# Five groups of split-number tiles begin 64 bytes further on in the on-chip memory

## The reference

```python
for layer in range(DEPTH):                    # 2
    if layer % 2 == 0:
        x = x + mixer_ab(x, ...)              # gated recurrence and pooling, then @ w_out (1536 rows)
    else:
        x = x + conformer_conv(x, ...)        # @ w1, depthwise conv, layer norm, silu, then @ w2
    x = x + cross_attn(x, mem, ...)           # 4 heads over 256 memory rows, then @ wo
    x = x + conv_ffn(x, ...)                  # (gelu(conv(h @ w_up)) * (h @ w_up')) @ w_down
return rms_norm(x, final_norm)
# second part: x + gated(rwkv7 mixer, 2D neighbourhood attention) @ w_out, then + experts
```

## The kernel before

| tiles | before | after |
|---|---|---|
| xg_hi, xg_lo, w_raw, w_hi, w_lo, mix_y, mix_z | 64 | 64 |
| f_h_hi, f_h_lo (2 layers, 2 of each), f_z, f_g, f_u | 0 | 64 |
| xa_o_hi, xa_o_lo (2 layers) | 0 | 64 |
| c_s_hi, c_s_lo, c_t1, c_t2, c_stack, c_w, c_rows, c_mem | 0 | 64 |
| ab_y_hi, ab_y_lo, ab_xr, ab_zr, ab_gate, ab_ga, ab_tmp and the other ab tiles | 0 | 64 |
| xa_m, xa_k, xa_v, xa_q, xa_p, xa_pT, c_h, c_mu, c_inv | 0 | 0 (128 bytes further on) |

## Time and profile before

### The profile page before, as it was taken

How to read it: one execution, slowest core, us unless ns; L and a number is a source line. 1 busy time by engine, 2 the same in 40 slices (tenths; PEclk the granted TensorE clock), 3 DMA queues, 4 the chain that set the end, 5 groups by cost and what they waited for, 6 DMA issues and landing times.

```text
span 2556.1 us, 40898 instructions
## 1 busy us (share of the span) xinstructions
PE 2450.5 (96%) x17480; PEld 1844.4 (72%) x17480; DVE 1341.0 (52%) x1870; ACT 922.7 (36%) x1278; POOL 239.6 (9%) x204
## 2 busy tenths in 40 slices
PE   8998999999999989999999999999999999899996
PEld 6777878888887657878888887877777777633332
DVE  6786546545456856545454556674466545511112
ACT  4454334333233235334232344334555543411110
POOL 1002000000000011010000011000111102133331
PEclk9999999999999999999999999999999999999998
DMA  5223222222223432222222223524212123599994
GB/s 185 89 74 111 103 94 83 100 98 99 99 98 115 131 103 99 99 83 99 99 99 99 84 98 129 199 97 165 72 41 57 40 98 135 198 371 379 380 397 169
DMA packets 100563, 343.20 MB, mean 134 GB/s; under 512 B 41376, under 2 KB 49952, under 8 KB 66592
## 3 DMA queue, kind: packets, MB, share of 16 engines
q1 hardware_dynamic: 86560, 332.15, 36.1%
q0 software_dynamic: 13824, 8.44, 1.1%
HBM read 368.32 MB, written 30.93 MB: 156 GB/s over the span
## 4 chain that ended last, share of the span: by engine, by line
PE 86%; DVE 6%; ACT 3%; issue 2%; DMA 2%; SPq 0%; POOL 0%; DVEq 0%; ACTq 0%; POOLq 0%
PE bank L572 83%; DVE w_lo L559 1%; PE bank L3225 1%; ACT w_hi L555 1%; DVE square L1978 1%; PE bank L2537 1%; DMA w_raw<-stream 1%; ACT rw_LT L2642 0%; PE bank L2405 0%; PE bank L3247 0%; SPq L1584 0%; DMA xa_mem<-mem_in 0%; DMA x<-x_spill 0%; PE bank L1367 0%; DMA e_w_raw<-y_rows 0%
## 5 line engine op out<-in xcount | busy, mean ns | idle before, releaser
L572 PE MATMUL bank<-xg_hi,w_hi 128*128 128x512 f32 x1568 | 620.3, 399 | 12.1 <-DVE xg_lo L596 12.1
L572 PE MATMUL bank<-xg_hi,w_lo 128*128 128x512 f32 x1536 | 600.5, 391 | 0.0
L572 PE MATMUL bank<-xg_lo,w_hi 128*128 128x512 f32 x1504 | 587.4, 391 | 0.0
L559 DVE TENSOR_TENSOR w_lo<-w_raw,w_hi 128x2048 fp32r<-128x2048 f32 x165 | 379.7, 2302 | 191.1 <-ACT w_hi L555 190.8
L555 ACT ACTIVATE w_hi<-w_raw 128x2048 fp32r<-128x2048 f32 x165 | 314.5, 1906 | 239.5 <-PE bank L572 210.3
L572 PEld LDWEIGHTS bank<-xg_hi,w_hi 128*128 128x128 f32 x1568 | 295.1, 189 | 84.0 <-DVE w_lo L559 12.1
L572 PEld LDWEIGHTS bank<-xg_hi,w_lo 128*128 128x128 f32 x1536 | 289.6, 189 | 61.0
L572 PEld LDWEIGHTS bank<-xg_lo,w_hi 128*128 128x128 f32 x1504 | 283.5, 188 | 62.7 <-issue 4.9
L572 PE MATMUL bank<-f_h_hi,w_hi 128*128 128x512 f32 x384 | 151.4, 394 | 0.0
L572 PE MATMUL bank<-f_h_hi,w_lo 128*128 128x512 f32 x384 | 150.6, 392 | 0.0
L572 PE MATMUL bank<-f_h_lo,w_hi 128*128 128x512 f32 x384 | 149.2, 388 | 0.0
(11 more groups left out here) (491 smaller groups left out, 4078.9 us busy)
## 6 DMA issues: line engine op xcount, KB each, us to landing
w_raw<-stream SPq DMA_DIRECT2D x165, 1024.0 KB, 4.8
e_over_ring<-expert_rows SPq DMA_DIRECT2D x70, 1024.0 KB, 10.2
e_w_raw<-expert_rows SPq DMA_DIRECT2D x26, 1024.0 KB, 9.8
p_spill<-p_stage SPq DMA_DIRECT2D x36, 256.0 KB, 2.1
na_bias<-bias_na SPq DMA_DIRECT2D x32, 160.0 KB, 4.4
mix_gate<-p_spill SPq DMA_DIRECT2D x16, 256.0 KB, 5.2
e_w_raw<-y_rows SPq DMA_DIRECT2D x8, 512.0 KB, 7.3
rw_rkv<-p_spill SPq DMA_DIRECT2D x12, 256.0 KB, 6.1
```

Of the source, the lines that this page charges most:

```text
L559: V.tensor_tensor(ring(m)["lo"][m % SLOTS][:, :], ring(m)["raw"][m % RAW][:, :], ring(m)["hi"][m % SLOTS][:, :].bitcast(F32), ALU.subtract ...
L572: return T.matmul(out_ap, lhsT, rhs, start=first, stop=last, skip_group_check=True)
```

## The change

Seven tiles of 16 float32 (64 bytes per partition) that nothing uses are placed: one ahead of the tiles of each stage of the first part (first mixer, each cross attention, with the convolution's tiles in the second, each feed-forward), and one between the attention's output and the tiles behind it. What begins at a multiple of 128 bytes now begins 64 bytes behind one, or, behind a second such tile, 128 bytes further on. No instruction is added, removed or moved on any engine, and no wait changes.

```diff
     with ExitStack() as ph:
+        sb(ph, "ab_first", [P, 16])
         with ExitStack() as inner:
             ab_under_y = sb(inner, "ab_under_y", [P, 2, KT, S])
         ab_y_hi, ab_y_lo = sb(ph, "ab_y_hi", [P, KT, S], F32R), sb(ph, "ab_y_lo", [P, KT, S], F32R)
...
     with ExitStack() as ph:
-        m = {"o_hi": sb(ph, "xa0_o_hi", [P, KT, S], F32R), "o_lo": sb(ph, "xa0_o_lo", [P, KT, S], F32R),
-             "m_hi": sb(ph, "xa0_m_hi", [P, KT, N_MEM], F32R), "m_lo": sb(ph, "xa0_m_lo", [P, KT, N_MEM], F32R),
+        sb(ph, "xa0_first", [P, 16])
+        m = {"o_hi": sb(ph, "xa0_o_hi", [P, KT, S], F32R), "o_lo": sb(ph, "xa0_o_lo", [P, KT, S], F32R)}
+        sb(ph, "xa0_between", [P, 16])
+        m |= {"m_hi": sb(ph, "xa0_m_hi", [P, KT, N_MEM], F32R), "m_lo": sb(ph, "xa0_m_lo", [P, KT, N_MEM], F32R),
              "k": sb(ph, "xa0_k", [P, 2, 2, N_MEM])}
...
     with ExitStack() as ph:
+        sb(ph, "xa1_first", [P, 16])
         with ExitStack() as conv:
...
         m = {"o_hi": sb(ph, "xa1_o_hi", [P, KT, S], F32R), "o_lo": sb(ph, "xa1_o_lo", [P, KT, S], F32R)}
+        sb(ph, "xa1_between", [P, 16])
         with ExitStack() as inner:
             c_h = sb(inner, "c_h", [P, KT, S])
...
         with ExitStack() as ph:
+            sb(ph, f"f{l}_first", [P, 16])
             with ExitStack() as inner:
                 f_under_h = sb(inner, f"f{l}_under_h", [P, KT + 3, S])
```

## The result

| | before | changed |
|---|---|---|
| median of 13 runs | 2553.10 us | 2560.23 us |
| lowest to highest | 2548.0 to 2556.5 | 2557.33 to 2563.34 |
| profiled execution, span | 2556.1 us | 2558.3 us |

A forecast was written before the change was run, and what follows sets the result against it. The prediction took PE's matmul pace as the bound; gains of 2.65 + 0.89 + 0.40 + 0.45 = 4.39, say 4.4 us, off 2555.46 gave 2551.1 us, with an 8-in-10 range of 2547.5 to 2555.5.

The forecast's parts named there:

- PE as the bound: Whole kernel: PE is busy for 96% of the span, so only the pace of its matmuls counts.
- The counts (1152, 384, 192, 288): Matmuls gaining in feed-forwards, attention outputs, convolution output and first mixer: 2.65, 0.89, 0.40 and 0.45 us.
- a third: First mixer: waits for VectorE take part of the 0.67 us gain, leaving two thirds, 0.45 us.
- the start is the one thing I find that splits them so: Seven 128x512 matmul families: starts at a multiple of 128 take 229 ns a step, 64 behind one 226.6.
- The slow end of the range: Upper end of the 8-in-10 range, 2555.5 us, set at the case of no change.
- The bad side: Moved tiles all at mix_z's slower 231.4 ns a step, costing 4.8 us over 2016 matmuls.
- The first rival: All moved tiles: something else about them, such as addresses against the weights, keeps 229.0 ns; 2555.5 us, chance 0.11.
- Tiles that end up 128 bytes further on (xa_m, xa_k, xa_q and the rest) begin as before: 0: Attention tiles behind a second gap: no change of pace, 0 us.
- The 16-byte line: SBUF reads: a penalty only on crossing 16-byte lines would give both starts equal pace, sum 0.
- The start-to-start of 215.7 ns: 512-column matmuls: reaching this documented pace would give 26.8 us; the prediction gave it no share.
- The clock as a rival: Pauses fall elsewhere and add half-clock stretches over busy PE: two cost 6.8 us, giving 2557.9 us; chance 0.05.

The follow-up runs named there:

- the feed-forwards alone: Kernel before with the 64-byte gap at the two feed-forwards only: median 2556.3 us against 2552.4, ratio 1.0014.
- the shift by 192: Kernel before with 192 bytes ahead of each first-part stage and 64 behind the attention's output: median 2549.17 us against 2553.49, ratio 0.9984.
- the second of the kernels with other starts: Kernel before with first-part stages shifted by 32 and 384 (feed-forwards), 448 and 96 (attentions), 192 bytes (first mixer): 2561.13 us beside 2552.4.

## Why the prediction was wrong, point by point

PE as the bound, and its pace as the only thing at stake: right. In the three kernels that were run many times (the change, the feed-forwards alone, the shift by 192) the time moved as the steps did, within the interval. Only in the first mixer did waits take up what the steps moved, in the profiled pair all of it, where the prediction had given them a third.

The counts (1152, 384, 192, 288) and the method, start to start over long runs: right as far as means go. The mean hid that the three f_h matmuls stand at 231.7, 229.2 and 225.9 ns, one of them below the 226.6 that was taken for the best pace.

The step that failed is "the start is the one thing I find that splits them so", with the starts taken modulo 128. The rows were right: three families at 226.6 and four at 229. Their reading was wrong in two things. First, the three families at 226.6 share one start modulo 256 (64), and the four at 229.0 another (128), so the trace could not tell a rule of period 128 from one of 256. The change's 64 bytes lead not towards the place of the three but away from it: from distance 64 to 128, where xg lies at 0, and from 229.0 to 233.3 ns a step for f_h. A gap of 192 closes the distance, as the run with it shows. Second, the start alone decides nothing. It is the distance to the weights, as the shift of everything and the shift of the weights show.

The slow end of the range was wrong with it. The bad side was taken from one odd place of mix_z at 231.4 ns and priced at 4.8 us slower, but the range ended at no change, since the long runs counted for more than those 8 matmuls. They showed no slower pace because no family of 512 columns lay at distance 128.

The first rival had the cause, "where their addresses lie against those of the weights over a longer period than 128 bytes", and then gave it the price of no change. It should have had both signs: if a longer period decides, 64 bytes lead to a place that the trace does not show.

"Tiles that end up 128 bytes further on (xa_m, xa_k, xa_q and the rest) begin as before: 0" was wrong for the same reason. xa_m went from a start of 128 to 0 modulo 256, and the 384 matmuls that have it as the stationary side lost about 3 ns each, 1.2 us.

The 16-byte line of the Trainium skill's page "SBUF — State Buffer", section "SBUF: two separate sides", gave no difference between any two of these starts. The runs show 226.7 to 234.3 ns among starts that are all multiples of 16, so it does not describe this. The start-to-start of 215.7 ns in the Trainium skill's page "TensorE: Matmul & The Clock Gate", section "Wait — 56ns, not 53.3ns?", was reached as the mean step at none of the ten distances tried.

The clock as a rival: no share. The stretches give 0.99 and 0.97 in both kernels.

## What to carry to other kernels

When rows fall into two groups by an address, write down the whole addresses of both groups, and of both operands, before naming a rule. A trace in which all cases of the better pace share one place cannot tell which modulus, or which operand, matters, and a shift that meets them only modulo n may lead to a place that it does not show. Here, the moving tile and both weight tiles of a float32r matmul of 512 columns belong at the same start modulo 256 bytes; it is worth 2.3 ns a matmul against distance 64 (1% of its step) and 6.6 against most others (3%).

A mean over a repeating group of three can hide unlike members: look at each member before taking the mean for the pace of one.

## What the runs showed of the hardware

For matmuls of 512 columns, among the ten distances tried, one place is best (0, at 226.7 ns) and 64 is second (229.0); 16 bytes beside the best already cost 5 ns. Matmuls of 256 columns do not share the optimum. With w as the moving and xa_m as the stationary side the median duration is 277 ns in the kernel before, where the moving start is 64 below the stationary one, and it is 283 in the second of the kernels with other starts:

```profile
L580 PE MATMUL bank<-w_hi,xa_m_hi x128: 278/283/471, 253.9 to 1108.8; 128*128 128x256 f32 x128
```

There the first attention's memory tiles lie at distance 0 and the second's at 96, and both have steps of 119.9 ns, against 114.7 before. With every tile shifted by 64 the steps are 114.7 and 113.6, so here too the start alone does not decide; but with the weights moved, and both sides 64 apart as before, they are 114.6 and 116.7, so the distance is not all of it.
